# Two transformer blocks on one core: the same four attention beats in every stage, and the pool inputs of the second block projected first

## The chip, the cores and the metric

The program runs on one core of one Trainium2 chip. The core has TensorE (PE in the profile, with its weight loads as PEld), VectorE (DVE), ScalarE (ACT), GpSimd (POOL) and SyncE (SP, which here only issues transfers). Each engine works through its own list of instructions in order and waits on semaphores for the others. The metric is the device time of the whole program in microseconds.

## The reference

The input is one sequence of 512 tokens with 1024 features. A first block has three attention branches that are gated and merged, and an MLP; then a second block runs twice (two layers), each a SwiGLU, a mixer with three branches, and another SwiGLU. What the change touches are the attention stages and the projections beside them:

```
# first block
oa = diff_attention(...)      # p0 - lam * p1, 4 heads of two parts
ob = banded_attention(...)    # window of 128, with a sink
oc = nsa_attention(...)       # compressed + selected + windowed branch, gated
# second block, for each of two layers
ya = chunked_relpos_attention(qa, ka, va, ..., rel_bias)
yb = multiscale_pool(ub, w_pool, pool_scale)       # windows 2, 4, 8, 16
yc = forgetting_attention(qc, kc, vc, ..., f_lin + forget_bias)
branch = einsum('bsnw,nwd->bsnd', stack([ya, yb, yc]), w_branch)
merged = sum(sigmoid(g) * branch)
```

## The kernel before, in words

Everything stays in SBUF transposed (features on partitions, 512 tokens in a row); weights stream in from memory through eight buffers. Products are made in three passes of single rounded parts: GpSimd splits each weight piece into `w_hi` and `w_lo` (L1119, L1122), and TensorE runs three matmuls for each block of 128 rows (L1151 to L1153). A "group" is one 128-column output: 8 such blocks, 24 matmuls, put down in pieces of two blocks (6 matmuls), so that other work can stand between pieces.

One list, `ORDER`, is written by `plan()` before the program is built. Each engine's program walks this list and emits its own part of every step. So the list fixes the order on every engine.

Attention runs as a pipeline over "duos" (two heads, one block of 128 queries). Stages in order of time: `att_a` (98 to 239 us of the trace, 16 duos), `att_b` (239 to 349 us, 16 duos), `att_c` (349 to 592 us, 48 duos, since each of the 16 has three branches), and for each layer of the second block `att_a2` (first layer 1502 to 1690 us) and `att_c2` (first layer 1690 to 1852 us), 16 duos each. A duo n goes through these steps:

- score: PE makes the scores (L1224) into banks 0 and 1, once the row maxima of duo n-1 are taken; DVE adds the bias and takes maxima (L1597) and negates them (L1602); ACT exponentiates (L1379).
- prob: DVE inverts the row sums (L1608) and scales the rows (L1634).
- turn: PE transposes the probabilities (L1241) into banks 2 and 3.
- copy: ACT moves them to SBUF, `pt_sb` (L1394). There is one `pt_sb`, so this waits for the pv of duo n-1.
- pv: PE multiplies by the values (L1266, L1253, L1261) into bank 4.
- At the last duo of a pair, bank 4 is moved out: `bout` is an ACT copy of the high part (L1467) and a DVE subtraction for the low part (L1812); in `att_a` it is a square and copy on ACT (`new_root`, "differential"). The pv of the next pair waits for that.

`attend()` returns a list of beats, each with a weight, and `weave()` deals out pieces of projection groups between beats in proportion to the weight. A "normed" group (query or key projection) is followed by a chain: square on ACT (L1353), a sum over channels on PE (L1210, into bank 5), a square root on ACT (L1361), two half reciprocals on DVE (L1557) and the scaled result on DVE (L1572). Only this last step gives the group's own bank back. `late()` holds these steps and lets one go after each piece. A "plain" or "token" group is just copied out by ACT.

Groups and pool products take banks in turn from a small ring: `MIX_RINGS` gives (6, 7) for `att_a2`, `att_c`, `att_c2`, and (3, 6, 7) for `att_a`, `att_b`. A pool product (`pool_steps`, PE L1323) also takes a place in the ring.

In `layer()` the stage `att_a2` has 17 groups: f (8 columns, for the forget gate), four u groups (pool input), four q and four k (normed), four token groups of values. `forget` is a small chain ACT, DVE, ACT in which ACT stands still while DVE works (L1412 to L1418, L1744 to L1753). `pool_steps` gives shifts, a last step (DVE) and a product.

Of the kernel before, what the change touches and what calls it, by code (L numbers as in the profile page):

```python
# [73 lines left out]
def put(*step):  # L74
    ORDER.append(step)
# [412 lines left out]
def attend(kind, layer):  # L488
# [20 lines left out]
    def turns(j):  # L509
        if 0 <= j + 1 < n:  # L510
            u = duos[j + 1]
            u.t_before = [take(b) for b in (T_BANKS[:1] if kind in ("att_a", "att_b") else T_BANKS)]
            for b in T_BANKS[:len(u.t_before)]:
                HELD[b] = ("pt_copied", u.n)
            put("turn", u)

    def products(j):
        if 0 <= j:
            u = duos[j]
            if u.first:  # L520
                u.o_before = take(O_BANK)
            u.need_v = READY[V_AT[kind]]
            put("pv", u)
        if 0 <= j and duos[j].last:
            u = duos[j]
            if kind == "att_a":
# [9 lines left out]
                masks.remove(e)  # L536
                mask_bias(e[1])

    def copy(j):
        if 0 <= j + 1 < n:  # L540
            put("copy", duos[j + 1])

    def scale(j):
        if j + 2 < n:
            put("prob", duos[j + 2])
# [1 line left out]
    out = []  # L547
    for j in range(-2, n):
        w = 1 + max([d.blocks for d in duos[max(0, j):j + 3]])
        if kind in ("att_b", "att_c", "att_c2"):  # L550
            out += [(lambda j=j: (scores(j), products(j)), 2 * w), (lambda j=j: (turns(j), copy(j)), w),
                    (lambda j=j: scale(j), w)]
        else:
            out += [(lambda j=j: scores(j), w), (lambda j=j: turns(j), w), (lambda j=j: (products(j), copy(j)), w),
                    (lambda j=j: scale(j), w)]
    return out + [(lambda: [mask_bias(b) for _, b in masks], 0)]


# [239 lines left out]
def layer(l, m):  # L798
# [12 lines left out]
    f = plain((l, "f"), ("f",), ring, width=8)  # L811
    q = [normed((l, "qc", i), "query", (l, 2), ("r2", i), ring) for i in range(4)]
    k = [normed((l, "kc", i), "key", (l, 3), ("r2", 4 + i), ring) for i in range(4)]

    steps = [pool_steps(g, ring) for g in range(4)]
    groups = [q[0], u[0], k[0], u[1], q[1], u[2], k[1], u[3], q[2], k[2], *token_groups((l, "vc"), S, "v1", ring),
              q[3], k[3]]
    jobs, chain = [f], []
    for g in groups:
        jobs += [g] + chain[:2]  # L820
        chain = chain[2:]
        if g is u[0]:
            jobs.append(forget)
        if g in u:
            shifts, product = steps[u.index(g)]
            chain += shifts + [product]
    jobs += chain
    weave("att_a2", l, jobs)
    ring = MIX_RINGS["att_c2"]
    weave("att_c2", l, merge((l + 1, 1), "br_b", "set", ring) + merge((l + 1, 0), "br_a", "mid", ring))  # L830
# [1161 lines left out]
```

How the kernel before makes its waits and increments, by code:

```python
    def wait_ge(self, name, n):  # L928
        if n > self.seen.get(name, 0):
            self.e.wait_ge(self.sem[name], n)
            self.seen[name] = n
# [1 line left out]
    def wait_at(self, at):  # L933
        if at:
            self.wait_ge(*at)
# [1 line left out]
    def settle(self):  # L937
        self.n += 1
        self.e.wait_ge(self.sem[self.chain], self.n)
# [139 lines left out]
        @block.sync  # L1080
        def _(sp):
            E = Engine(sp, sem, "out_done")
            for c in range(0, KC, 2):
                sp.dma_start(x[:, c, :], x_in[:, c, :]).then_inc(sem[f"x_loaded{c}"], 16)
            for p, piece in enumerate(PIECES):
                if p >= NR:
                    E.wait_ge("w_used", p - NR + 1)
                src = weights[AT[p] - piece.cols * P:AT[p]].rearrange("(p n) -> p n", p=P)
                sp.dma_start(raw[:, p % NR, 0:piece.cols], src).then_inc(sem[f"loaded{p % NR}"], 16)
            for d in range(KC):
                E.wait_ge("x_added", TOTAL["x_added"] - KC + d + 1)
                sp.dma_start(out[:, d, :], x[:, d, :]).then_inc(sem["out_done"], 16)
            sp.wait_ge(sem["out_done"], 16 * KC)
# [17 lines left out]
            def split(h):  # L1111
                p = SPLITS[h]
                n = PIECES[p].cols
                piece, high = raw[:, p % NR, 0:n], w_hi[:, h % NH, 0:n]
                if h >= NH:
                    E.wait_ge("w_used", SPLITS[h - NH] + 1)
                E.wait_ge(f"loaded{p % NR}", 16 * (p // NR + 1))
                nc.gpsimd.tensor_tensor(high, piece, ones[:, 0:1].to_broadcast([P, n]), ALU.mult)\
```

## Time and profile before

| | us |
|---|---|
| median of 3 runs | 3600.44 (3597.36 to 3603.72) |
| the profiled execution, its own time | 3600.44 |
| its span, first to last instruction | 3598.6 |
| PE busy | 3435.6 (95%) |
| GpSimd busy | 2371.3 (66%) |
| DVE busy | 1427.4 (40%) |
| ACT busy | 772.4 (21%) |
| chain that ended last | PE 87%, DVE 8%, ACT 3%, issue 2% |

The chain that ended last is the path of instructions and waits that ends with the last instruction. A row of waits says which engine stood idle, before which line, and which line's end let it go. A timeline row gives start and length, then the engine, line and operation with output and inputs by name, and in brackets the idle time before it. The slices of the page show where PE is not full: the first six of forty slices (the first block's attention), and a short dip in each layer of the second block.

### The profile page before, as it was taken

The numbers are of one execution on the slowest core, as the hardware profiler recorded it, in microseconds if no ns is written. First come the engines' busy times: TensorE is split into PE (matmuls) and PEld (weight loads), VectorE is DVE, ScalarE is ACT, GpSimd is POOL, SyncE is SP. The second block draws the span as 40 slices with busy tenths as digits, with TensorE's granted clock in tenths as the row PEclk, the third lists the DMA queues.
The fourth block names the chain that finished last, engine by engine and source line by source line (L and its number), as shares of the span: only waits on it lengthen the run. The fifth ranks groups of instructions, "written<-read, shape, count | busy, mean of one in ns | idle before, by whom it ended". The sixth has DMA issues, their size and how long they took to land.

```text
span 3598.6 us, 42372 instructions
## 1 busy us (share of the span) xinstructions
PE 3435.6 (95%) x17034; PEld 2751.9 (76%) x17034; DVE 1427.4 (40%) x2757; ACT 772.4 (21%) x1568; POOL 2371.3 (66%) x1238
## 2 busy tenths in 40 slices
PE   7876999999999999989999999999999889999999
PEld 6554667888898888656779888888887567788887
DVE  5656564433453234565333111332345653332111
ACT  2544332211120002243212100210012432111000
POOL 6413445787768776644677877787775436688775
PEclk9988999999999999999999999999999999999999
DMA  3212122254525442211222322254432112232222
GB/s 138 66 59 71 59 65 80 96 210 164 187 104 223 171 164 100 77 59 59 94 94 94 106 97 96 88 205 168 165 129 71 65 50 89 79 106 94 99 94 76
DMA packets 104195, 388.08 MB, mean 108 GB/s; under 512 B 11824, under 2 KB 12080, under 8 KB 97856
## 3 DMA queue, kind: packets, MB, share of 16 engines
q1 hardware_dynamic: 87984, 292.76, 24.2%
q10 hardware_dynamic: 16016, 92.62, 6.7%
q8 instruction: 135, 2.21, 0.3%
q14 instruction: 60, 0.49, 0.0%
HBM read 383.20 MB, written 2.13 MB: 107 GB/s over the span
## 4 chain that ended last, share of the span: by engine, by line
PE 87%; DVE 8%; ACT 3%; issue 2%; DMA 0%; ACTq 0%; DVEq 0%
PE psum L1151 27%; PE psum L1152 26%; PE psum L1153 26%; PE psum L1224 2%; PE psum L1266 2%; PE psum L1241 2%; DVE rs_t L1557 2%; DVE s_sb L1597 1%; PE psum L1210 1%; ACT s_sb L1379 1%; DVE neg_max L1602 1%; DVE s_sb L1634 1%; ACT sq_t L1353 0%; DMA small<-first_small_dram 0%; ACT L1361 0%
## 5 line engine op out<-in xcount | busy, mean ns | idle before, releaser
L1119 POOL TENSOR_TENSOR w_hi<-raw,ones 128x1024 fp32r<-128x1024 f32 (+3 forms) x591 | 1043.0, 1765 | 1064.7 <-PE psum L1153 1055.5
L1122 POOL TENSOR_TENSOR w_lo<-raw,w_hi 128x1024 fp32r<-128x1024 f32 (+3 forms) x591 | 1314.5, 2224 | 46.5
L1151 PE MATMUL psum<-h_hi,w_hi 128*128 128x512 f32 (+2 forms) x2912 | 1143.5, 393 | 29.8 <-DVE r L1572 17.5
L1153 PE MATMUL psum<-h_hi,w_lo 128*128 128x512 f32 (+2 forms) x2912 | 1108.1, 381 | 0.0
L1152 PE MATMUL psum<-h_lo,w_hi 128*128 128x512 f32 (+2 forms) x2912 | 1107.9, 380 | 0.0
L1151 PEld LDWEIGHTS psum<-h_hi,w_hi 128*128 128x128 f32 (+1 forms) x2912 | 552.0, 190 | 167.2 <-issue 34.2
L1153 PEld LDWEIGHTS psum<-h_hi,w_lo 128*128 128x128 f32 (+1 forms) x2912 | 551.4, 189 | 106.6
L1152 PEld LDWEIGHTS psum<-h_lo,w_hi 128*128 128x128 f32 (+1 forms) x2912 | 552.7, 190 | 101.0 <-issue 6.3
L1151 PE MATMUL psum<-a_hi,w_hi 128*128 128x512 f32 (+1 forms) x1064 | 392.5, 369 | 0.0
L1152 PE MATMUL psum<-a_lo,w_hi 128*128 128x512 f32 (+1 forms) x1064 | 391.9, 368 | 0.0
L1153 PE MATMUL psum<-a_hi,w_lo 128*128 128x512 f32 (+1 forms) x1064 | 391.9, 368 | 0.0
L1824 DVE TENSOR_TENSOR psum<-g_sb,psum 128x512 f32<-128x512 f32 x120 | 83.5, 696 | 734.3 <-PE psum L1153 641.4
L1502 ACT ACTIVATE g_sb<-psum 128x512 f32<-128x512 f32 x120 | 71.7, 598 | 919.5 <-PE psum L1153 832.9
L1379 ACT ACTIVATE s_sb<-s_sb,neg_max 128x128 f32<-128x128 f32 (+6 forms) x272 | 140.7, 518 | 487.0 <-DVE neg_max L1602 486.9
L1833 DVE SCALAR_TENSOR_TENSOR x<-psum,res,x 128x512 f32<-128x512 f32 (+1 forms) x132 | 88.4, 669 | 357.6 <-PE psum L1153 357.6
L1557 DVE RECIPROCAL rs_t<-rs_t 128x256 f32<-128x256 f32 x110 | 187.2, 1730 | 101.5 <-ACT rs_t L1361 101.3
L1151 PEld LDWEIGHTS psum<-a_hi,w_hi 128*128 128x128 f32 x1064 | 200.6, 189 | 33.7
L1152 PEld LDWEIGHTS psum<-a_lo,w_hi 128*128 128x128 f32 x1064 | 200.6, 189 | 33.5
L1153 PEld LDWEIGHTS psum<-a_hi,w_lo 128*128 128x128 f32 x1064 | 200.6, 189 | 33.1
L1509 ACT ACTIVATE a_hi<-psum 128x512 fp32r<-128x512 f32 x120 | 71.8, 598 | 494.0 <-DVE psum L1824 494.0
L1597 DVE CUSTOM_DVE_ANT_0 s_sb<-psum,bias_t 128x128 f32<-128x128 f32 (+3 forms) x224 | 109.5, 489 | 169.5 <-PE psum L1224 119.6
L1695 DVE CUSTOM_DVE_ANT_0 ada_t<-ada_t,psum 128x1024 f32<-128x1024 f32 x144 | 167.7, 1215 | 0.0
(189 smaller groups left out, 3385.2 us busy)
## 6 DMA issues: line engine op xcount, KB each, us to landing
raw<-weights_dram SPq DMA_DIRECT2D x489, 512.0 KB, 3.4
ada_t<-ada_dram ACTq DMA_DIRECT2D x48, 1536.0 KB, 7.1
raw<-weights_dram SPq DMA_DIRECT2D x72, 256.0 KB, 2.6
raw<-weights_dram SPq DMA_DIRECT2D x32, 384.0 KB, 2.9
bias_t<-biases_dram ACTq DMA_DIRECT2D x36, 256.0 KB, 2.9
bias_t<-cum_dram ACTq DMA_DIRECT2D x16, 256.0 KB, 4.0
out_dram<-x SPq DMA_DIRECT2D x8, 256.0 KB, 2.0
raw<-weights_dram SPq DMA_DIRECT2D x4, 408.0 KB, 3.1
```

The lines of the kernel that those rows point to most:

```text
L1119: nc.gpsimd.tensor_tensor(high, piece, ones[:, 0:1].to_broadcast([P, n]), ALU.mult)\
L1122: nc.gpsimd.tensor_tensor(w_lo[:, p % NR, 0:n], piece, high.bitcast(F32), ALU.subtract)\
L1151: mm(dst, lh, rh, start=first, stop=False)
L1152: mm(dst, lh, rl, start=False, stop=False)
L1153: return mm(dst, ll, rh, start=False, stop=last)
L1224: ins = mm(bank(SCORE_BANKS[half], w), q, k, start=True, stop=u.kind != "att_c2")
L1379: ins = fn(to, s, ACT.Exp, bias=neg_max[:, r:r + 1], accum_out=row_sum[:, r:r + 1])
L1557: v.reciprocal(r, r).then_inc(sem["qk_inverse"], 1)
L1597: v.tensor_tensor_reduce(out=s[:, 0:w], in0=bank(SCORE_BANKS[half], w), in1=tile, scale=1.0, scalar=s[:, w:w + 1] if u.kind == "att_b" els ...
L1695: ins = v.tensor_tensor_reduce(out=part, in0=part, in1=c_bcast, scale=1.0, scalar=0.0, op0=ALU.mult, op1=ALU.add, accum_out=mod_raw[:, l, ...
L1824: v.tensor_tensor(bank(g.bank), g_sb[:, n % 2, :], bank(g.bank), ALU.mult)\
L1833: v.scalar_tensor_tensor(x[:, d, cs], bank(g.bank)[:, cs], res_of(which, d), x[:, d, cs], ALU.mult, ALU.add).then_inc(sem["x_added"], 1)
```

## The change

The first part is in `attend()`. Before, three kinds (`att_b`, `att_c`, `att_c2`) had three beats a duo: score of duo j+2 with pv of duo j, weight 2w; turn and copy of duo j+1, weight w; prob of duo j+2, weight w. The other two had four beats. Now all kinds have four: score, turn, pv, prob, each of weight w. And the copy of duo j+1 is put down inside `products`, right behind pv and ahead of what follows the last duo of a pair (`bout`, or the square and copy of `att_a`).

The second part is in `layer()`: the order of the 17 groups of `att_a2`. Before, u groups stood between q and k groups and the values ahead of q3 and k3. Now the order is f, u0, u1, u2, u3, q0, k0, q1, k1, q2, k2, q3, k3, and the four token groups, with the forget step behind u0 and the pool steps between groups from u1 on.

```
@@ attend
             put("pv", u)
+        if 0 <= j + 1 < n:
+            put("copy", duos[j + 1])
         if 0 <= j and duos[j].last:
...
-    def copy(j):
-        if 0 <= j + 1 < n:
-            put("copy", duos[j + 1])
...
         w = 1 + max([d.blocks for d in duos[max(0, j):j + 3]])
-        if kind in ("att_b", "att_c", "att_c2"):
-            out += [(lambda j=j: (scores(j), products(j)), 2 * w), (lambda j=j: (turns(j), copy(j)), w),
-                    (lambda j=j: scale(j), w)]
-        else:
-            out += [(lambda j=j: scores(j), w), (lambda j=j: turns(j), w), (lambda j=j: (products(j), copy(j)), w),
-                    (lambda j=j: scale(j), w)]
+        out += [(lambda j=j: scores(j), w), (lambda j=j: turns(j), w), (lambda j=j: products(j), w),
+                (lambda j=j: scale(j), w)]
@@ layer
-    groups = [q[0], u[0], k[0], u[1], q[1], u[2], k[1], u[3], q[2], k[2], *token_groups((l, "vc"), S, "v1", ring),
-              q[3], k[3]]
-    jobs, chain = [f], []
-    for g in groups:
-        jobs += [g] + chain[:2]
-        chain = chain[2:]
-        if g is u[0]:
-            jobs.append(forget)
-        if g in u:
-            shifts, product = steps[u.index(g)]
-            chain += shifts + [product]
-    jobs += chain
+    jobs = [f, u[0], forget, u[1], *steps[0][0], u[2], steps[0][1], *steps[1][0], u[3], steps[1][1]]
+    chain = [s for ss, prod in steps[2:] for s in ss + [prod]]
+    rest = [q[0], k[0], q[1], k[1], q[2], k[2], q[3], k[3]] + token_groups((l, "vc"), S, "v1", ring)
+    for i, g in enumerate(rest):
+        jobs.append(g)
+        jobs += chain[2 * i:2 * i + 2] if i < 11 else chain[2 * i:]
     weave("att_a2", l, jobs)
```

Lines of the changed kernel below its `layer()` stand 13 lower than before (L1210 is L1197, and so on).

**Place 1: `att_b`, end of its first pair, on PE.** L1224 is the score of duo 22, L1266 the pv of duo 20 (the last of its pair), L1210 the sum of a normed group, L1241 the turn of duo 21 (with the change L1211, L1253, L1197 and L1228). Before:

```order
L1224 MATMUL psum<-k_56,r_51 128x256 [waits row_max]
L1224 MATMUL psum<-k_56,r_51 128x256
L1266 MATMUL psum<-pt_sb,v_bc 64x128 [waits pt_copied]
L1266 MATMUL psum<-pt_sb,v_bc 64x128 x3
L1151 MATMUL psum<-h_hi,w_hi 128x512
L1152 MATMUL psum<-h_lo,w_hi 128x512
L1153 MATMUL psum<-h_hi,w_lo 128x512
L1151 MATMUL psum<-h_hi,w_hi 128x512
L1152 MATMUL psum<-h_lo,w_hi 128x512
L1153 MATMUL psum<-h_hi,w_lo 128x512
L1210 MATMUL psum<-sq_t,cst 128x512 [waits qk_rooted,qk_squared]
L1241 MATMUL psum<-cst,s_sb 128x128 [waits probs]
```

and with the change:

```order
L1211 MATMUL psum<-k_56,r_51 128x256 [waits row_max]
L1211 MATMUL psum<-k_56,r_51 128x256
L1228 MATMUL psum<-cst,s_sb 128x128 [waits pt_copied,probs]
L1228 MATMUL psum<-cst,s_sb 128x128 x3
L1138 MATMUL psum<-h_hi,w_hi 128x512
L1139 MATMUL psum<-h_lo,w_hi 128x512
L1140 MATMUL psum<-h_hi,w_lo 128x512
L1138 MATMUL psum<-h_hi,w_hi 128x512
L1139 MATMUL psum<-h_lo,w_hi 128x512
L1140 MATMUL psum<-h_hi,w_lo 128x512
L1197 MATMUL psum<-sq_t,cst 128x512 [waits qk_rooted,qk_squared]
L1253 MATMUL psum<-pt_sb,v_bc 64x128 x4
```

The pv of the pair's last duo stood right behind the score; now it stands behind the turn, a piece of the projection and the sum.

**Place 2: the same place on ACT.** L1467 (now L1454) is the first half of `bout`, L1394 (now L1381) the copy of duo 21, L1361 (now L1348) the square root of the normed group. Before:

```order
L1467 ACTIVATE br_b<-psum 128x512 [waits pv]
L1353 ACTIVATE sq_t<-psum 128x512 [waits w_used]
L1361 ACT_TABLE_LOAD
L1361 ACTIVATE rs_t<-psum,eps_t 128x512 [waits qk_summed]
L1394 ACTIVATE pt_sb<-psum 128x2x256 [waits transposed]
```

and with the change:

```order
L1340 ACTIVATE sq_t<-psum 128x512 [waits w_used]
L1348 ACT_TABLE_LOAD
L1348 ACTIVATE rs_t<-psum,eps_t 128x512 [waits qk_summed]
L1381 ACTIVATE pt_sb<-psum 128x2x256 [waits pv,transposed]
L1454 ACTIVATE br_b<-psum 128x512
```

The `bout` copy went from the front of this run to its end, behind the square, the table load, the root and the copy. Its DVE half (L1812) keeps its place in DVE's list, ahead of the scaling of duo 22.

**Place 3: `att_a2`, the third pool product (PE).** L1323 (now L1310) is the pool product, behind it the first matmuls of the next normed group, k2 before and k1 with the change. Before:

```order
L1210 MATMUL psum<-sq_t,cst 128x512 [waits qk_rooted,qk_squared]
L1241 MATMUL psum<-cst,s_sb 128x128 [waits pt_copied,probs]
L1241 MATMUL psum<-cst,s_sb 128x128 x7
L1323 MATMUL psum<-pool_d,lay 128x512 [waits plain_out,pool_in]
L1151 MATMUL psum<-h_hi,w_hi 128x512 [waits w_lo,qk_out]
L1152 MATMUL psum<-h_lo,w_hi 128x512
```

and with the change:

```order
L1197 MATMUL psum<-sq_t,cst 128x512 [waits qk_rooted,qk_squared]
L1253 MATMUL psum<-pt_sb,v_57 64x128 x8
L1310 MATMUL psum<-pool_d,lay 128x512 [waits qk_out,pool_in]
L1138 MATMUL psum<-h_hi,w_hi 128x512 [waits w_lo,qk_out]
L1139 MATMUL psum<-h_lo,w_hi 128x512
L1140 MATMUL psum<-h_hi,w_lo 128x512
```

In both, the group behind the product has the same bank (7) as the normed group ahead of it, since the product took bank 6 between them, and waits for `qk_out` (L1572) of that group. Before, the other three products stand behind a plain or token group. With the change the first two do, and the fourth stands behind k2, a normed group, with q3 behind it on k2's bank: the wait stands twice in each layer instead of once.

## Rows read from the trace of the kernel before

**Rows 1.** Busy time of each engine by stretch; PEclk is the granted clock

```profile
core 0: us, PE busy (x) PEld busy (x) DVE busy (x) ACT busy (x) POOL busy (x), PEclk, DMA share, GB/s
239.00:349.00 110.00, 76.67 (x422) 47.77 (x421) 69.59 (x181) 49.58 (x113) 33.20 (x28) 0.83 0.22 75
349.00:592.00 243.00, 228.28 (x1348) 161.35 (x1344) 145.50 (x466) 87.93 (x262) 107.85 (x72) 0.96 0.19 60
1502.00:1690.00 188.00, 161.99 (x785) 108.75 (x784) 112.48 (x210) 74.78 (x139) 86.11 (x47) 0.95 0.19 63
1690.00:1852.00 162.00, 160.81 (x866) 122.38 (x864) 60.80 (x141) 40.27 (x96) 101.90 (x65) 1.00 0.28 88
```

**Rows 2.** Waits of PE, 1502 to 1692 us: in total, times, longest

```profile
PE psum L1210 <- ACT sq_t L1353: 17.1, 8, 6.4
PE psum L1151 <- DVE r L1572: 6.5, 1, 6.5
PE psum L1224 <- DVE neg_max L1602: 1.6, 1, 1.6
PE psum L1241 <- DVE s_sb L1634: 0.8, 1, 0.8
```

**Rows 3.** Waits of PE, 239 to 349 us

```profile
PE psum L1241 <- DVE s_sb L1634: 6.9, 3, 3.2
PE psum L1266 <- ACT pt_sb L1394: 3.3, 5, 1.1
PE psum L1266 <- DVE br_b L1812: 2.4, 2, 1.6
```

**Rows 4.** Waits of PE, 349 to 592 us

```profile
PE psum L1241 <- DVE s_sb L1634: 7.0, 6, 2.3
PE psum L1266 <- ACT pt_sb L1394: 2.3, 3, 1.3
PE psum L1253 <- ACT pt_sb L1394: 1.2, 2, 0.7
PE psum L1266 <- DVE br_c L1812: 1.1, 2, 0.7
```

**Rows 5.** Timeline of ACT in that stretch: start, length, idle before it

```profile
1532.03 0.61 ACT L1412 ACTIVATE f_t<-f_t 8x512 f32<-8x512 f32 x1
1539.10 0.60 ACT L1394 ACTIVATE pt_sb<-psum 128x512 f32<-128x512 f32 x1 [3.79 <-DVE f_t L1753]
```

**Rows 6.** Timeline of ACT and DVE behind one query or key group

```profile
1584.22 0.60 ACT L1353 ACTIVATE sq_t<-psum 128x512 f32<-128x512 f32 x1 [1.29 <-PE psum L1153]
1584.83 1.28 ACT L1361 ACT_TABLE_LOAD   x1
1586.13 0.69 ACT L1361 ACTIVATE rs_t<-psum,eps_t 128x512 f32<-128x512 f32 x1
1586.92 1.75 DVE L1557 RECIPROCAL rs_t<-rs_t 128x256 f32<-128x256 f32 x1 [3.20 <-ACT rs_t L1361]
1591.01 0.75 DVE L1572 SCALAR_TENSOR_TENSOR r<-psum,lay,rs_t 128x512 f32<-128x512 f32 x1
```

**Rows 7.** DVE's L1602, 1502 to 1690 us: busy, mean ns; then shortest/median/longest

```profile
L1602 DVE TENSOR_SCALAR neg_max<-row_max 128x2 f32<-128x2 f32 x18 | 11.1, 614 | 0.6
L1602 DVE TENSOR_SCALAR neg_max<-row_max x18: 168/169/1848, 1503.6 to 1687.8; 128x2 f32<-128x2 f32 x18
```

**Rows 8.** Busy time by stretch, right behind three of PE's waits

```profile
1519.50:1524.00 4.50, 4.44 (x15) 3.14 (x16) 1.83 (x2) 1.98 (x3) 4.42 (x3) 0.62 0.01 5
1616.00:1619.00 3.00, 3.00 (x10) 1.91 (x10) 0.55 (x2) 0.00 (x0) 0.00 (x0) 0.53 0.00 0
1626.00:1629.00 3.00, 2.60 (x12) 1.82 (x12) 2.34 (x3) 2.32 (x3) 2.92 (x2) 1.00 0.70 251
```

**Rows 9.** Timeline of PE, one turn in that stretch

```profile
425.09 0.87 PE L1241 MATMUL psum<-cst,s_sb 128*128 128x128 f32 x6 [2.28 <-DVE s_sb L1634]
```

**Rows 10.** Timeline of DVE, the first subtraction of that stretch

```profile
279.24 0.69 DVE L1812 TENSOR_TENSOR br_b<-psum,br_b 128x512 fp32r<-128x512 f32 x1 [1.64 <-ACT br_b L1467]
```

## The prediction, made before the changed kernel ran

> **What bounds the kernel now.** I read the busy time by stretch first. TensorE is full nearly everywhere: in `att_c2` it works 160.8 of 162 us, so nothing about waits can be won or lost there [rows 1]. The change touches only the attention stages, and three kinds of them have room: `att_b` (76.7 of 110 us busy), `att_c` (228.3 of 243) and `att_a2` (162.0 of 188, once per layer) [rows 1]. Then I asked each of these for PE's waits. In `att_a2` they are 17.1 + 6.5 + 1.6 + 0.8 = 26.0 us a layer: eight waits of a group's channel sum for its square on ACT, the longest 6.4, and one of 6.5 for a bank that a normed group still holds [rows 2]. In `att_b` and `att_c` the turn waits for scaled probabilities (6.9 and 7.0) and the pv for its copy or for the output bank (3.3 + 2.4 and 2.3 + 1.2 + 1.1) [rows 3, 4]. Last comes what stands around these waits on ACT and DVE. Elsewhere the program is word for word the same.
>
> **Part 1, the order of groups in `att_a2`.** No instruction is added; 17 groups of 24 matmuls, 16 duos, 8 sums and 4 pool products stay. Only waits change.
>
> What goes. The 6.4 us wait is ACT standing in `forget`: it starts at 1532.03 and the copy behind it at 1539.10, 7.1 us, and the square of k0 is queued behind that and one duo's exponentials [rows 5]. With the change the group in that place is a plain one: no square, no sum. PE meets forget through the copy of duo 82 and the probabilities of duo 83, with a whole group (4 pieces of about 1.5), a pv and a score between, about 7.4 us. DVE's scaling of duo 83 stands behind forget's scan and takes 0.8; I leave 1.2 us (bounds 0 and 6.4). The 1.6 us at the stage's end goes, since the last normed group is four token groups earlier.
>
> What comes. First the waits at the start: 0.8 as before, 1.2 for forget, and 0.5 each where u3 and q0 take the bank of the plain group ahead, 3.0 together. Each of eight normed groups costs at least 0.7, the square of 0.60 and the hand-over [rows 6]: 5.5. Now eight of them stand in a row, so I set the chain against PE's slot. From a group's end: square 0.60, table load 1.28, root 0.69, half reciprocal 1.75, one duo's scaling 0.8, the other half 1.75, result 0.75 [rows 6], then a duo's maxima (0.8 to 1.7) and exponentials (0.9 to 1.5), and only then the next square: 9.3 to 10.8 us. PE's slot (wait, sum, four pieces, one score, turn and pv) is 9.1 to 10.5. In four slots chain and slot meet within 0.3; in three, where a score has no turn behind it or a subtraction stands between, walking through the list gives 2.2, 1.2 and 1.2. With 0.3 for the others that is 4.9.
>
> Then the bank. A wait on a normed group's bank now comes twice. From the group's end the result is out after about 7.5 us (the same chain without maxima and exponentials), and PE has 3.7 us of sum, pv or turn, and pool product in front: 3.8 each, 7.6 (bounds 2 and 6.5, the latter the wait of before [rows 2], which had a late square ahead of it).
>
> GpSimd splits weights all the time, and the little negation of two columns takes 169 ns or up to 1848, 614 in the mean [rows 7]. It is on the chain in each slot: 8 x (0.614 - 0.169) = 3.6.
>
> Sum of waits: 3.0 + 5.5 + 4.9 + 7.6 + 3.6 = 24.6 against 26.0. The clock comes on top. Behind the long waits PE's granted clock is between its two levels (1.2 and 2.4 GHz): 0.62 over 4.5 us, 0.53 over 3 us, after waits of 2.4 and 6.5; after one of 1.8 it is 1.00 [rows 8]. That is 1.7 and 1.4 us lost. Before there are four such waits, 6.2 us; after I count three (two banks and the 2.2 with its 0.7), 4.7. So 29.3 against 32.2: 2.9 less in a layer, 5.8 less in both. Bounds: without lateness and contention 16.1 + 3.1, 13 less in a layer; with bank waits of 6.5 and twice the contention 6 more.
>
> **Part 2, the beats in `att_b`, `att_c`, `att_c2`.** Two things follow. The turn of duo j+1 comes earlier after its probabilities: pv of duo j, and in many duos a piece of the projection, no longer stand between. Against that the pv comes later after its copy, and those waits go.
>
> `att_c`: I took each of the 48 turns, the time between its probabilities and its start, and the work that is moved behind it (0.4 to 2.4 us). In twelve of them the work is more than that time; the extra waits add up to 8.4. The largest is 2.2, the turn at 425.09, which waits 2.28 already [rows 9]; the others are 0.2 to 1.1. The pv waits of 2.3 + 1.2 + 1.1 = 4.6 go [rows 4]: 3.8 more.
>
> The output subtraction. It stands in DVE's list ahead of a duo's scaling, and waits for ACT's `bout` copy, that waits for the pair's last pv. Before, that pv is right behind the score, and the subtraction starts at 279.24 after 1.64 us of waiting [rows 10]. Now turn, projection piece and at the first pair of `att_b` also a channel sum stand ahead on PE, and square, load, root and copy on ACT. Walking on, the pv ends near 281.1, copy and `bout` near 282.4, the subtraction near 283.1: 3.2 us later than 279.93, where its end was. DVE's list slips with it. At other pairs it is 0.5 to 1.2 in `att_b`, where the exponentials hold ACT anyway, and up to 3 in `att_c`, where most disappears in slack. For `att_b`, where PE waits on DVE, I take 2.0 + 0.5 + 1.2 = 3.7 and nothing for its turns (they fall into other waits on DVE) nor for pv waits. For `att_c` I take 2.5 besides the 3.8: 6.3. Bounds: -3 to +8 and -3 to +14.
>
> `att_c2`: the turns have 3.8 us or more and lose at most 3.8; nothing. `att_a`: the copy, 0.60 [rows 5], now stands ahead of the square at a pair's end; four times, mostly beside a projection piece: 1.0 (0 to 2.4). GpSimd's and SP's lists don't change but for the places of masks, that nobody waits for; the order in which weights come follows the groups, at the same bytes.
>
> **Sum.** -5.8 + 3.7 + 6.3 + 1.0 = +5.2. The profiled execution took 3600.4 us, 1.8 more than its span, and is the median itself. So 3605.6; I say 3605.
>
> **A rule weighed.** In [rows 6] the load ends at 1586.11 and the root begins at 1586.13. The Trainium skill, "ScalarE: Activation LUTs", section "What ACT_TABLE_LOAD costs", states 1.28 us and a drain of 1.38 on top for each switch. By that page's figures, an estimate, each chain of the eight in a row would be 1.4 longer, about 20 us over two layers. The load agrees with the trace, the drain doesn't show in it, and this gets no chance.
>
> **The rivals.**
> A, faster: the projections win. Chains stay inside PE's slots, as four of eight group ends in `att_a2` now cost only 0.7, and contention misses them: -13 a layer. For it speaks that slots and chain are equal within a microsecond; against it that [rows 7] has a mean three times the shortest. With half of part 2 (5): 3600.4 - 26 + 5 = 3579.
> B, slower: the subtraction decides. If each of the eight pair ends in `att_b` and `att_c` costs the 3.2 of the first, it is 26 instead of 6.2: 3605 + 20 = 3625. It decides from the point where the next scaling has less than 3.2 us before its turn; in [rows 9] it has none. Against it: DVE is busy only 60% of these stretches.
> C, slower: GpSimd on DVE's chain in `att_a2`. At the longest row, 1.68 more each of eight times, it is 13.4 instead of 3.6, 20 us over both layers: 3625; with half of the slots 3615. The Trainium skill, "SBUF — State Buffer", section "SBUF: two separate sides", has the port pair as an exclusive lock held for a whole instruction, by which such a hit lasts to the end of GpSimd's; the longest row fits.
> D: the waits in part 2 only change places, and it nets to nothing: 3600.4 - 5.8 + 1 = 3596.
>
> **How the numbers follow.** A measurement here can tell 0.2%, 7.2 us, from nothing: 3593 to 3608. My forecast and D lie in it, together 0.40. A has 0.22, B 0.24, C 0.14. So faster 0.22, same 0.40, slower 0.38. The range takes in most of A's way down and B and C: 3586 to 3625; the forecast's own is 3596 to 3613.
>
> **What would show it.** In `att_a2`: no 6.4 us wait behind forget, two waits on `r` (L1559 of the changed kernel) near 3.8, eight waits for squares, three of them above 1.5, a stage of about 185 us. In `att_b`: the first subtraction (L1799) near 282.4 instead of 279.2. In `att_c`: pv waits gone, turn waits near 13. I am wrong if the bank waits are gone or above 6, if `att_c` gets shorter, or if `att_c2` moves at all.

## The result, and the profile after

The changed kernel takes 3640.2 us (median of 4, 3638.3 to 3644.3) against 3601.6 (3597.4 to 3603.7) for the kernel before in the same session: ratio 1.011, 95% interval 1.0093 to 1.0128. It is slower, and outside the range I gave (3586 to 3625). The profiled execution took 3637.6 us, with a span of 3635.8.

Busy time by stretch in the changed kernel, in order of time: `att_a`, `att_b`, `att_c`, and the first layer's `att_a2` and `att_c2`, cut where each one's first score starts:

```profile
core 0: us, PE busy (x) PEld busy (x) DVE busy (x) ACT busy (x) POOL busy (x), PEclk, DMA share, GB/s
98.70:236.30 137.60, 112.95 (x521) 82.03 (x520) 92.19 (x178) 71.28 (x137) 52.91 (x35) 0.96 0.20 63
236.30:353.30 117.00, 75.13 (x423) 46.19 (x422) 72.75 (x180) 49.03 (x111) 33.19 (x28) 0.85 0.20 69
353.30:608.00 254.70, 234.83 (x1346) 158.69 (x1344) 156.62 (x466) 88.36 (x263) 107.89 (x72) 0.97 0.18 58
1519.50:1705.50 186.00, 154.25 (x739) 102.93 (x738) 103.07 (x196) 74.93 (x135) 77.34 (x41) 0.93 0.17 58
1705.50:1878.60 173.10, 171.89 (x914) 127.98 (x912) 70.73 (x155) 42.37 (x102) 111.64 (x71) 1.00 0.28 88
```

Set against the kernel before, in us. Each stage begins at its first score and lasts to that of the next; `att_c` and `att_c2`, behind which other work follows, end with their last pv (so `att_c2` is 1.6 shorter here than its window above):

| stage | before | after | change |
|---|---|---|---|
| `att_a` | 141.2 | 137.6 | -3.6 |
| `att_b` | 109.3 | 117.0 | +7.7 |
| `att_c` | 242.9 | 254.7 | +11.8 |
| `att_a2`, two layers | 176.2, 174.7 | 186.0, 185.9 | +9.8, +11.2 |
| `att_c2`, two layers | 170.6, 170.6 | 171.5, 171.5 | +0.9, +0.9 |

They add up to 38.7; the spans differ by 37.2, and what lies between the stages is 1.5 shorter. All but `att_a` came out positive.

How far can a single stage length be trusted? `att_b` and `att_c` have the same program in the changed kernel and in three runs that come below, `e1`, `e7` and `r9`. There `att_b` takes 119.7, 119.8 and 119.8 instead of 117.0, and `att_c` 254.6, 259.4 and 254.8 instead of 254.7. The waits are the same (41.9 to 42.1 us in `att_b` in all four); what differs is PE's busy time in `att_b` (75.1 against 77.7) with the granted clock of the stretch (0.85 against 0.83). So a stage length can be off by 3 us or more for the clock alone, while the sums of waits nearly repeat (with the old program of `att_b` 33.3 before, 33.4 in `e3` and 32.6 in `o1`), and the loss of `att_b` is nearer 10 than 7.7.

PE's waits in `att_a2` of the changed kernel (total, times, longest), the counterpart of [rows 2]:

```profile
PE psum L1138 <- DVE r L1559: 12.8, 2, 7.1
PE psum L1197 <- ACT sq_t L1340: 11.1, 8, 3.7
PE psum L1228 <- DVE s_sb L1621: 7.5, 3, 6.1
```

31.4 us, against 24.4 in the same cut before (the 26.0 of [rows 2] has a wait of 1.6 behind it, which belongs to `att_c2`). The waits for squares fell from 17.1 to 11.1, as meant. But the bank waits are 7.1 and 5.6 where I had 3.8 each, and the turn behind forget waits 6.1 (I had 1.2). PE's busy time rose too, from 151.8 to 154.3 with the same 739 matmuls: behind the waits of 6.1 and 7.1 the 512-column matmuls take 0.63 us instead of 0.39. In `att_b` and `att_c` (two queries, against [rows 3, 4]):

```profile
PE psum L1228 <- DVE s_sb L1621: 16.4, 8, 6.1
PE psum L1211 <- DVE neg_max L1589: 9.0, 4, 6.2
PE psum L1197 <- ACT sq_t L1340: 8.7, 4, 6.1
PE psum L1297 <- ACT cmp_g L1460: 7.8, 1, 7.8
```

```profile
PE psum L1228 <- DVE s_sb L1621: 13.9, 10, 4.7
PE psum L1211 <- DVE neg_max L1589: 3.1, 1, 3.1
PE psum L1226 <- DVE s_sb L1621: 2.8, 2, 1.8
```

Before, `att_b` also had these beside those of [rows 3], and `att_c` the same wait of 3.1 for its first row maxima:

```profile
PE psum L1224 <- DVE neg_max L1602: 11.3, 5, 6.2
PE psum L1310 <- ACT cmp_g L1473: 5.3, 1, 5.3
PE psum L1210 <- ACT sq_t L1353: 4.1, 4, 1.6
```

The waits of pv are gone in both. In `att_b` all waits together rose from 33.3 to 41.9: turns 9.5 more, squares 4.6 more, the last row (the gate of the next stage) 2.5 more, scores 2.3 less and pv 5.7 less. In `att_c` the turns wait 16.7 instead of 7.0, and all waits together rose from 14.7 to 19.8 us. This rise of 5.1 is less than half of the stage's 11.8. The rest is busy time: the PE column of its window is 234.8 instead of 228.2, with the same 1346 matmuls and a granted clock that is no lower (0.97 against 0.96). A view of waits alone doesn't show that.

### The profile page after: what moved, and what is told of

The parts are those of the page before. It is cut to its first block, busy times and chain, and to the rows that moved or that the text cites. A ratio compares the mean times of both kernels' runs of the same rounds, so it can differ in the third digit from the quotient of the medians.

```text
span 3635.8 us, 42471 instructions
## 1 busy us (share of the span) xinstructions
PE 3447.4 (95%) x17034; PEld 2746.0 (76%) x17034; DVE 1442.9 (40%) x2757; ACT 777.5 (21%) x1572; POOL 2373.3 (65%) x1238
## 3 DMA queue, kind: packets, MB, share of 16 engines
q1 hardware_dynamic: 87984, 292.76, 23.6%
## 4 chain that ended last, share of the span: by engine, by line
PE 86%; DVE 8%; ACT 3%; issue 2%; DMA 0%; ACTq 0%; DVEq 0%
PE psum L1138 27%; PE psum L1139 26%; PE psum L1140 26%; PE psum L1211 2%; PE psum L1253 2%; PE psum L1228 2%; DVE rs_t L1544 2%; DVE s_sb L1584 1%; PE psum L1197 1%; ACT s_sb L1366 1%; DVE neg_max L1589 1%; DVE s_sb L1621 1%; ACT sq_t L1340 0%; DMA small<-first_small_dram 0%; ACT L1348 0%
## 5 line engine op out<-in xcount | busy, mean ns | idle before, releaser
L1138 PEld LDWEIGHTS psum<-h_hi,w_hi 128*128 128x128 f32 (+1 forms) x2912 | 552.5, 190 | 191.0 <-issue 41.9
L1139 PEld LDWEIGHTS psum<-a_lo,w_hi 128*128 128x128 f32 x1064 | 200.6, 188 | 33.3
L1140 PEld LDWEIGHTS psum<-a_hi,w_lo 128*128 128x128 f32 x1064 | 200.5, 188 | 33.3
L1584 DVE CUSTOM_DVE_ANT_0 s_sb<-psum,bias_t 128x128 f32<-128x128 f32 (+3 forms) x224 | 109.4, 488 | 173.3 <-PE psum L1211 126.0
```

What stands on the lines that cost most here:

```text
L1138: mm(dst, lh, rh, start=first, stop=False)
L1139: mm(dst, lh, rl, start=False, stop=False)
L1140: return mm(dst, ll, rh, start=False, stop=last)
L1584: v.tensor_tensor_reduce(out=s[:, 0:w], in0=bank(SCORE_BANKS[half], w), in1=tile, scale=1.0, scalar=s[:, w:w + 1] if u.kind == "att_b" els ...
```

## The experiments

All stage lengths below are cut as in the table above, and each is from one execution. Each ratio is against the kernel before in the same session (its medians were 3598.9 to 3600.5). Everything not named is as in the kernel that a run starts from.

### Which part, which stage

`e1_beats_alone` has the new beats and the old groups, `e2_groups_alone` the new groups and the old beats. `e3_copy_in_a` moves only the copy in `att_a` and `att_a2`:

```
             put("pv", u)
+        if kind in ("att_a", "att_a2") and 0 <= j + 1 < n:
+            put("copy", duos[j + 1])
```

`e4_beats_old_copy` has the four beats with the copy where it was, `e5_pv_first_even` four even beats with pv ahead of the turn (the lines are shortened):

```
-            out += [(lambda j=j: (scores(j), products(j)), 2 * w), (lambda j=j: (turns(j), copy(j)), w), ...
+ e4         out += [(scores, w), (turns, w), (products and copy, w), (scale, w)]
+ e5         out += [(scores, w), (products, w), (turns and copy, w), (scale, w)]
```

> Part 2 and the early copy alone: four beats of equal weight in all five kinds, the copy right behind pv; groups of att_a2 in their old order. Theory (the parts add up): att_a 137.6 us, att_b 117.0, att_c 254.7, att_c2 173.1 as in the changed kernel, att_a2 near 176; sum 3600 - 3.6 + 7.7 + 11.7 - 1.0 = 3615, ratio 1.004. Rival (the two parts only hurt together, since the place of groups and beats against each other decides): under 3605, with att_c below 248.

> The new order of groups in att_a2 alone, beats as before. Theory (the parts add up): att_a2 near 186 us in both layers, its forget wait near 6 and its two bank waits near 7 and 5.6 stay; 3600 + 21 = 3621, ratio 1.006. Rival (the early copy makes the forget wait, as the copy of duo 83 then stands in front): forget wait under 3, att_a2 near 180, 3608.

> Only the copy's place in the two four-beat kinds att_a and att_a2: right behind pv, ahead of the square of a pair's end. Theory: att_a 137.6 us instead of 141.2, att_a2 within 1 of 176.2; 3597, ratio 0.999. Rival (the gain in att_a came from something else, such as the phase of GpSimd's splits): att_a within 1 of 141.2, 3600.

> Four beats in att_b, att_c, att_c2, but the copy behind the output copy as before, in all kinds; old order of groups. Theory (the turn moved ahead of the piece and of pv decides, not the copy): att_b near 117, att_c near 254, att_a 141.2; 3619, ratio 1.005. Rival (the place of the copy ahead of the output copy delays the subtraction and makes the loss): att_b near 110, att_c near 244, 3601.

> The kernel before with four equal beats in att_b, att_c and att_c2, but pv still ahead of the turn (score, pv, turn and copy, prob, one weight each). It tells the order from the spread of the pieces. Theory (what costs is that a turn stands ahead of pv, so that it comes sooner after its probabilities): att_b 109 to 111, att_c 242 to 245, att_c2 170.6; 3600 to 3604. Rival (the equal spread of the projection's pieces costs, whichever of the two comes first): att_b near 114, att_c near 254, 3613.

| run | us; ratio, 95% interval | `att_a` | `att_b` | `att_c` | `att_a2` | `att_c2` |
|---|---|---|---|---|---|---|
| before | 3600.0 | 141.2 | 109.3 | 242.9 | 176.2, 174.7 | 170.6 |
| e1 | 3623.2; 1.0063 (1.0048 to 1.0078) | 138.7 | 119.7 | 254.6 | 176.2, 176.8 | 173.1 |
| e2 | 3614.9; 1.0040 (1.0025 to 1.0055) | 137.9 | 109.4 | 242.3 | 185.1, 186.3 | 169.0 |
| e3 | 3602.4; 1.0004 (0.9994 to 1.0014) | 143.5 | 109.8 | 243.0 | 177.6, 174.7 | 170.6 |
| e4 | 3613.1; 1.0041 (1.0028 to 1.0054) | 137.9 | 113.6 | 253.9 | 174.8, 174.8 | 173.1 |
| e5 | 3607.5; 1.0016 (1.0006 to 1.0025) | 137.9 | 115.9 | 243.2 | 176.5, 174.9 | 173.2 |

The parts add: 0.63% and 0.40% make 1.03% of the 1.1%. The rival of e1 fell, though e1 came out 8 us above the 3615 that I had added up from single stage lengths, and e2 6 us below its 3621. The rival of e2 fell too: without the early copy, forget's wait is still 6.1 and the bank waits 7.1 and 5.6.

The 3.6 of `att_a` is no effect of the change that these runs could show. The stage has the same program before and in e2, e4 and e5, and takes 141.2 us in the first and 137.9 in the other three; e3 with the copy moved takes 143.5. My expectation for e3 missed. With its program unchanged the length ranges from 137.2 to 144.7 over the runs here, and the granted clock from 98.5 to 236 us is 0.96 in the shortest (o2), 0.93 before, and 0.89 in the longest (o1).

In `att_c` the order decides. The copy's place is worth 0.7 (e4, 253.9), within the scatter, the even spread 0.3 (e5); the turn ahead of pv is worth 10.7. In `att_b` it is the other way round, and there I go by the waits, since they repeat: 33.3 before, 38.8 in e5, 38.9 in e4 and 42.1 in e1. So the even spread makes 5.5, the turn ahead of pv nothing, and the early copy 3. Here the rival of e5 was right, and the theory of e4 (near 117) missed. `att_c2` takes 2.5 from the beats and gives 1.6 back with the groups, as the wait at its start goes.

### The wait behind forget

`e7_forget_in_four` starts from the changed kernel:

```
-    jobs = [f, u[0], forget, u[1], *steps[0][0], u[2], steps[0][1], *steps[1][0], u[3], steps[1][1]]
+    jobs = [f, u[0], lambda: forget(0), u[1], *steps[0][0], lambda: forget(1), u[2], steps[0][1], *steps[1][0],
+            lambda: forget(2), u[3], steps[1][1], lambda: forget(3)]
```

> The changed kernel with forget cut into four steps at four places (sum and ACT's three functions behind u0; DVE's three small operations ahead of u2; the scan ahead of u3; ACT's store behind u3). Theory (the 6.1 us wait is DVE's scan in front of a scaling, and ACT's wait for it inside forget in front of a copy): the wait goes to under 2, att_a2 185.9 to about 179 in each layer with the clock behind it; 3640 - 13 = 3627. Rival (the wait is GpSimd on DVE's port, which meets whatever operation stands there): at least 4 of the 6.1 stay, in the scaling or the scan; 3636.

Measured: 3627.5 us, 1.0071 (1.0056 to 1.0086), `att_a2` 179.1 and 178.8: 6.9 and 7.1 less than in the changed kernel. The turn behind forget doesn't wait any more, two later ones wait 0.3 and 0.4, and a bank waits 1.9 for ACT. The time is the theory's. But that the wait goes when the operations stand apart doesn't say why they took so long together, and there the rival had a part. DVE's timeline of the changed kernel shows it (start, length, operation), with two rows of GpSimd behind it:

```profile
1540.02 2.40 DVE L1734 TENSOR_SCALAR f_t<-f_t 8x512 f32<-8x512 f32 x1 [4.44 <-ACT f_t L1403]
1542.45 0.68 DVE L1736 TENSOR_TENSOR f_t<-f_t 8x512 f32<-8x512 f32 x1
...
1543.88 2.08 DVE L1740 TENSOR_TENSOR_SCAN f_t<-f_t 8x512 f32<-8x512 f32 x1
...
1546.05 2.46 DVE L1621 TENSOR_SCALAR s_sb<-s_sb,row_inv 128x256 f32<-128x256 f32 x2
1542.52 2.37 POOL L1106 TENSOR_TENSOR w_hi<-raw,ones 128x1024 fp32r<-128x1024 f32 x1 [0.38 <-PE psum L1140]
1544.96 3.13 POOL L1109 TENSOR_TENSOR w_lo<-raw,w_hi 128x1024 fp32r<-128x1024 f32 x1
```

The first took 0.41 before, the scan 1.21, and the scaling is 0.62 where nothing stands against it. The three are 4.7 longer, and my 1.2 plus 4.7 is 5.9 of the 6.1 measured. But for 0.4 us ahead of 1542.52, GpSimd splits weights in all this time. With the splits made short (e8, next) the same turn waits 0.8, for ACT, though forget stands whole. So the 6.1 needs both: three operations in a row, and GpSimd beside them.

### GpSimd against DVE

`e8_after_short_splits` and `e9_before_short_splits` make the two split operations short, in the changed kernel and in the one before. They leave out the low part of the weights: TensorE reads the high part in its place, with as many matmuls, waits and transfers:

```
-                n = PIECES[p].cols
+                n = PIECES[p].cols if h < 24 else 32
-                nc.gpsimd.tensor_tensor(w_lo[:, p % NR, 0:n], piece, high.bitcast(F32), ALU.subtract)\
+                nc.gpsimd.tensor_tensor(rest[:], piece[:, 0:32], high[:, 0:32].bitcast(F32), ALU.subtract)\
-                        wh, wl = w_hi[:, h % NH, w], w_lo[:, p % NR, w]
+                        wh, wl = w_hi[:, h % NH, w], w_hi[:, h % NH, w]
```

> The changed kernel with GpSimd's two split operations cut to 32 columns (the high part is kept from the first pieces, the low part is left out and the high one read in its place): GpSimd is all but idle, every wait and every transfer stays. With the next kernel it tells how much of the change's loss is GpSimd on DVE. Theory G (GpSimd's hits make a third or more of it): changed less before comes to under 26 us instead of 38; att_c differs by under 7 instead of 11.8, att_a2 by under 7 instead of 10 to 11, and forget's wait is near 2. Theory O (the order of PE alone): the differences stay as they are within 2 us.

> The kernel before with the same short splits (the same part left out). Both theories: DVE's operations of 0.2 us are never 1 us or longer, and the kernel is faster than 3600 by what GpSimd costs it: by the DVE waits of PE in the attention stages 20 to 60 us. Theory G: it gains less from this than the changed kernel does, 12 us or more less; theory O: both gain the same.

| | `att_b` | `att_c` | `att_a2` | `att_c2` | all |
|---|---|---|---|---|---|
| e9, before, short | 102.4 | 230.2 | 165.6, 165.1 | 169.9 | 3570.7 |
| e8, after, short | 104.5 | 239.4 | 174.6, 173.2 | 170.7 | 3597.4 |
| difference | 2.1 | 9.2 | 9.0, 8.1 | 0.8 | 26.7 |
| with full splits | 7.7 | 11.8 | 9.8, 11.2 | 0.9 | 38.6 |

Against its own session the kernel before is 30 us faster with short splits, the changed one 43. That is a net number: in the profiled executions the seven attention stages together are 48 us shorter in e9 and 58 in e8, but the rest of the program is 19 and 17 us longer, though PE is full and hardly waits there. Why is open, so the two runs are not a clean removal of GpSimd. Of the change's loss the splits make 12 us: 5.6 of 7.7 in `att_b`, 2.6 in `att_c`, and 0.8 and 3.1 in `att_a2`. Theory G just missed its own signs (26.7 where it wanted under 26, 31% where it wanted a third), and missed by stage, where I had expected under 7 in `att_c` and `att_a2`; theory O, that nothing changes by more than 2, missed by far more (the changed kernel gains 13 us more than the other, G's 12 or more). The bank waits are the same to 0.1 with short splits, so they come from the order of the lists:

```profile
PE psum L1139 <- DVE r L1560: 12.7, 2, 7.1
PE psum L1198 <- ACT sq_t L1341: 10.0, 8, 2.6
```

Which of DVE's operations are hit? Two lines of equal size in the kernel before, all 144 duos (duration min/median/max in ns):

```profile
L1602 DVE TENSOR_SCALAR neg_max<-row_max x144: 168/170/2222, 99.9 to 3099.5; 128x2 f32<-128x2 f32 x144
L1608 DVE RECIPROCAL row_inv<-row_sum x144: 99/165/167, 101.8 to 3103.7; 128x2 f32<-128x2 f32 x144
```

The reciprocal is never longer than 167 ns; the negation goes up to 2222. Counted in the trace, the negation started inside a running split 60 times and was lengthened by over 0.4 us in 42 of them. The length says more: all 53 that started with over 0.17 us of the split to go ended 22 to 30 ns behind the split's end, and the 84 that started outside of a split took 172 ns at most. So the operation waits for the end of GpSimd's. Of the scalings by `row_inv` (L1634), those of 128 and 256 columns were lengthened 28 times in 28, those of 384 and 512 in 14 of 20. The reciprocals (L1608, L1557) were never lengthened in 106 such starts, nor was `scalar_tensor_tensor` with an input in PSUM (L1543) in 89. The Trainium skill, "SBUF — State Buffer", section "SBUF: two separate sides", names the operations that take part in the lock on the port pair that the two engines share: a DVE operation in a 2-port mode or with two inputs in SBUF. The trace agrees as far as these kinds go.

In `att_b` two hits in a row show how it comes about. DVE and GpSimd in the changed kernel, from 331 us:

```profile
331.77 2.32 DVE L1621 TENSOR_SCALAR s_sb<-s_sb,row_inv 128x256 f32<-128x256 f32 x2
...
335.26 1.13 DVE L1589 TENSOR_SCALAR neg_max<-row_max 128x2 f32<-128x2 f32 x1
332.05 1.89 POOL L1106 TENSOR_TENSOR w_hi<-raw,ones 128x1024 fp32r<-128x1024 f32 x1 [15.09 <-PE psum L1140]
334.02 2.35 POOL L1109 TENSOR_TENSOR w_lo<-raw,w_hi 128x1024 fp32r<-128x1024 f32 x1
```

The piece of the projection ends at 331.97, which frees GpSimd's slot; its split starts at 332.05, inside a scaling that takes 2.32 instead of 0.62, and the next catches the negation (1.13 for 0.17). ACT's exponentials and the square behind them slip, and the channel sum waits 6.1 us. In e8 the same wait is 3.5, shorter by the 2.6 that the two hits add.

### The negation on ACT

`r12_before_negation_on_act`:

```
-                v.tensor_scalar(neg_max[:, r:r + 2], row_max[:, r:r + 2], -1.0, None, ALU.mult)
+                fn(neg_max[:, u.at:u.at + 2], row_max[:, u.at:u.at + 2], ACT.Copy, scale=-1.0)   # in exps()
```

> The kernel before with the negation of the maxima (two columns, 0.17 us or up to 1.8 on DVE) moved to ACT, in all 144 duos. Theory (this little operation waits for the end of a GpSimd split in 42 of 144 cases, 47 us in all, and a part of it is on PE's path): DVE's excess falls by over 40 us, PE's waits in att_b, att_c and att_a2 by 8 to 15; 3588. Rival (what DVE is spared there, its next scaling or ACT's extra operation, 0.2 us each, pays): 3598 to 3606.

Measured: 3602.1 us, 1.0004 (0.9996 to 1.0013). The rival was right. DVE's excess, each operation's time above the median of its line and shape, fell from 143 to 106 us: the negations' 47 went, and the scalings behind them were hit harder (58 to 64). But PE gained nothing by it in sum. `att_c` is 4.1 shorter, `att_a2` 1.1 and 2.2 longer, and there the added operation stands on ACT, for whose squares PE waits. What part of the rest each of the two pays was not told apart.

### The banks behind a product

DVE in the changed kernel behind the longest bank wait, and ACT's operation ahead of it:

```profile
1602.25 0.69 ACT L1518 ACTIVATE br_b<-psum,lay 128x512 fp32r<-128x512 f32 x1 [0.60 <-PE psum L1310]
1602.97 0.75 DVE L1835 SCALAR_TENSOR_TENSOR br_b<-psum,lay,br_b 128x512 fp32r<-128x512 f32 x1 [5.41 <-ACT br_b L1518]
1603.64 0.14 DVE L1707 COPY pool_s<-r 128x1 f32<-128x1 f32 x1
1603.82 0.69 DVE L1709 TENSOR_TENSOR pool_s<-r 128x511 f32<-128x511 f32 x1
1604.54 1.75 DVE L1544 RECIPROCAL rs_t<-rs_t 128x256 f32<-128x256 f32 x1
...
1606.75 1.75 DVE L1544 RECIPROCAL rs_t<-rs_t 128x256 f32<-128x256 f32 x1
1608.54 0.75 DVE L1559 SCALAR_TENSOR_TENSOR r<-psum,lay,rs_t 128x512 f32<-128x512 f32 x1
```

The root of the group whose bank PE waits for was done at 1600.95. DVE took it up at 1604.54: its list has the product's output (L1835) and a pool shift ahead of the reciprocals, and L1835 waits for PE's product and ACT. That is 3.6 us on top of the chain I had walked, and with my 3.8 it makes 7.4 for the 7.1 measured.

`r9_products_late`, from the changed kernel:

```
-    chain = [s for ss, prod in steps[2:] for s in ss + [prod]]
+    chain = steps[2][0] + steps[3][0]
...
-        jobs += chain[2 * i:2 * i + 2] if i < 11 else chain[2 * i:]
+        jobs += chain[2 * i:2 * i + 2]
+        if i in (8, 10):
+            jobs.append(steps[2 + (i == 10)][1])
```

`r10_before_forget_in_four` splits forget in the kernel before. `r11_groups_repaired` takes the old beats, the new groups, r9's products and e7's forget.

> The changed kernel with pool products 2 and 3 moved from the run of normed groups to the token groups; their shifts stay where they are. Theory (a product takes one of the two banks, so that the next normed group has to take that of the group just ended, and DVE's list has the product's output, which waits for PE and ACT, ahead of that group's reciprocals): both bank waits, 7.1 and 5.6, go, and with them the low clock behind them; att_a2 185.9 to 170 to 173 in each layer, 3640 - 28 = 3612. Rival (the chain of square, root, reciprocals is as long as PE's slot, so the time comes back as later squares): waits for squares rise by 5 or more, att_a2 179 to 183, 3630.

> The kernel before with forget in four steps (behind u0, k0, u1 and q1). Theory (the 6.4 us wait is ACT held in forget by its wait for DVE's scan): it goes to under 1.5, att_a2 176.2 to 168 to 171 with the clock behind it; 3600 - 12 = 3588, ratio 0.997. Rival (DVE, lengthened by GpSimd, then delays the scaling instead): att_a2 above 173, 3596.

> The beats of before, the new order of groups, with products 2 and 3 late and forget in four steps: both causes of att_a2's loss taken away. Theory: att_a2 186 - 6.9 - 14 = 165 in each layer against 176.2 and 174.7 of before; 3600 - 20 = 3580, ratio 0.9945. Rival (eight normed groups in a row are dear in themselves): att_a2 172 or more, 3595.

| run | us | ratio, 95% interval | `att_a2` |
|---|---|---|---|
| r9 | 3614.9 | 1.0041 (1.0028 to 1.0054) | 172.1, 172.0 |
| r10 | 3593.1 | 0.9979 (0.9970 to 0.9988) | 172.7, 171.3 |
| r11 | 3572.6 | 0.9928 (0.9915 to 0.9940) | 162.5, 162.6 |

r9's theory holds: 13.9 us a layer, and the squares rose by 0.8, not 5. It takes away two things at once, the product's turn on the bank ring and its output in DVE's list, and no run parts them; the 3.6 above is the share that the timeline gives to the list. r10 gave less than expected: the wait of 6.4 is 1.8, but a bank waits 1.8 and a turn 1.1 behind it. r11 beats both kernels. PE's waits in its `att_a2`:

```profile
PE psum L1210 <- ACT sq_t L1353: 11.9, 8, 3.7
PE psum L1151 <- ACT r L1370: 1.9, 1, 1.9
PE psum L1241 <- DVE s_sb L1637: 1.5, 3, 0.8
```

Against r10, which has the old order of groups and forget in four too, r11's `att_a2` is 10.2 and 8.7 shorter. So the order of groups is good; it was the two steps inside it that cost.

### PE's own time

Three rows of `att_c`, first e5 (pv first), then e4 (turn first), then e8 (turn first, short splits); the fourth is e9, the kernel before with short splits:

```profile
352.40:595.60 243.20, 229.80 (x1346) 158.72 (x1344) 152.50 (x466) 87.47 (x262) 107.90 (x72) 0.97 0.20 60
350.00:603.90 253.90, 234.69 (x1346) 158.61 (x1344) 157.65 (x466) 88.42 (x262) 107.96 (x72) 0.98 0.19 58
336.70:576.10 239.40, 231.62 (x1346) 156.96 (x1344) 111.49 (x466) 89.09 (x262) 18.30 (x69) 0.99 0.20 61
336.30:566.50 230.20, 224.10 (x1346) 159.04 (x1344) 111.18 (x466) 88.97 (x262) 18.17 (x68) 0.99 0.21 64
```

The same 1346 matmuls keep PE busy 4.9 longer if turns stand first, and 7.5 longer in e8 than in e9, where its waits differ by 2.0 (7.7 and 5.7 summed). I cut the trace of `att_c` into runs of matmuls of one kind, from a run's first start to the next run's first start, idle time off: before, the 48 turns take 18.5, after 23.6; the pieces 150.5 and 152.4 (in 83 and 90 runs); scores and pvs together 59.3 and 58.9. Before, 46 of 48 turns had a piece behind them, after 24, and 24 a pv. Turns of equal size show the same: a turn of two matmuls takes 0.14 us between two pieces (e5 and e4), 0.19 to 0.20 with a score or pv ahead and a piece behind, 0.32 with a piece ahead and a pv behind, and 0.39 with a score ahead and a pv behind.

`att_c2` has hardly a wait, so it was the place to tell apart the number of visits and what follows what:

```
+        if kind == "att_c2":
+ o1         out += [(lambda j=j: (scores(j), turns(j), products(j), copy(j), scale(j)), 4 * w)]
+ o2         out += [(lambda j=j: (scores(j), products(j), turns(j), copy(j), scale(j)), 4 * w)]
```

> The kernel before, in att_c2 alone one beat of weight four: score, turn, pv in a row, then all of the duo's pieces. Theory V (PE pays 0.09 us for each separate visit, as 28 more of them made 2.5): one visit a duo instead of two, att_c2 168 us instead of 170.6 in each layer. Theory N (it pays by which follows which; a turn in front of pv is dearer than one in front of a piece by about 0.12): 171 to 175.

> The same with score, pv, turn in a row. Theory V: 168 us, as with the turn first. Theory N: 170 to 171, 1 us or more less than with the turn first.

```profile
1678.40:1849.00 170.60, 167.85 (x903) 127.62 (x901) 69.30 (x157) 42.81 (x102) 101.48 (x66) 1.00 0.26 82
1688.80:1861.90 173.10, 170.37 (x909) 127.05 (x907) 71.07 (x157) 43.22 (x102) 102.91 (x66) 1.00 0.27 82
1683.40:1852.40 169.00, 167.11 (x903) 127.54 (x901) 73.49 (x157) 41.43 (x102) 101.93 (x66) 1.00 0.27 83
1674.90:1843.10 168.20, 166.32 (x903) 127.61 (x901) 74.93 (x157) 41.38 (x102) 101.67 (x66) 1.00 0.27 83
```

In this order: before (33 runs of pieces in the stage), e4 (47), o1 (17, turn first) and o2 (17, pv first). PE is busy 167.9, 170.4, 167.1, 166.3. But the matmul counts say that e4's stage isn't the same work: 909 against 903 in the others, one piece of six matmuls more before the last pv, and at 0.23 us each (the distance of two in the timeline) that is 1.4 of the 2.5. That piece is then missing behind the stage. From the first score of `att_c2` to that of the next `att_a2` the kernel before takes 1094.9 us, e4 1094.6 and the changed kernel 1094.4; from the second `att_c2` to the end it is 650.6, 651.6 and 650.0. So 14 more visits cost 1.1 in the stage (by the landmarks nothing in the first layer, 1.0 in the second), and 16 fewer in the same order (o2) give 1.5: 0.1 us each or a little less, and the change as a whole loses nothing there. The order counts as well: 15 turns in front of a pv cost 0.8 (o1 against o2). Each theory had half. o2 is 3591.4 us, 0.9980 (0.9970 to 0.9990), o1 0.9993 (0.9983 to 1.0003). In `att_c`, where the counts are equal, the order costs more, 4.9 for 24 turns; why four times as much per turn stays open. The profile models the ends of matmuls, and some of it may be short waits that hide under them.

`o3_repaired_and_negation` is r11 with r12's negation in `att_c` alone.

> The repaired kernel (beats of before, new groups, products late, forget in four steps) with the negation of the maxima on ACT in att_c alone. Theory (it took 4.1 us from att_c in the kernel before): 3568, att_c 238.7. Rival (another phase of GpSimd's splits against DVE gives it back): 3573.

Measured: 3570.8 us, 0.9919 (0.9905 to 0.9932). `att_c` is 240.8, not 238.7: 1.7 less than in r11, and by the total it can't be told from r11 (nor can its theory, 3568, be told from its rival, 3573).

## Why the prediction was wrong

The sum was +5.2 and is +38.6. Step by step:

- **`att_a2`, -2.9 a layer; measured +9.8 and +11.2.** (Of the 2.9, 1.6 was the last wait of [rows 2], which went and is counted in `att_c2` here.) The squares were a little better than forecast: 14.0 forecast with contention, 11.1 measured, three of eight above 1.5. The step that failed is "3.8 each" for the bank waits (12.8 instead of 7.6). I had walked the normed group's chain and not DVE's list, in which the product's output stands ahead of it and waits for two other engines. The second failed step is the 1.2 for forget: its cover is right with short splits (the turn waits 0.8 for its copy there in e8, and DVE's three operations take 0.41, 1.21 and 0.62), but three operations in a row were hit. Third, the clock: I had it give 1.5 back, and PE's busy time rose by 2.5, since the long waits were four (6.1, 7.1, 3.7 and 5.6) where I had counted three shorter ones. I had said that I am wrong if the bank waits are above 6, and one is.
- **Contention.** Rival C had GpSimd on the negations of eight chains. DVE's excess in `att_a2` fell instead, from 22 to 14 us. Three of the hits went to forget and the scaling behind it, where each counted.
- **`att_b`, +3.7; measured +7.7.** The mechanism is there. The first subtraction starts 42.6 us behind the stage's start instead of 39.5: 3.1 later, where I had worked out 3.2:

```profile
278.89 0.69 DVE L1799 TENSOR_TENSOR br_b<-psum,br_b 128x512 fp32r<-128x512 f32 x1 [4.62 <-ACT br_b L1454]
```

  With short splits the loss is 2.1, and in the full kernels the two hits at 331.77 and 335.26 make 2.6 of it. The term that was too small is the waits: 3.7 forecast, 8.6 measured, the turns behind DVE's list above all.
- **`att_c`, +6.3; measured +11.8.** The size of the waits was right: 5.1 more, the pv waits gone, turn waits 16.7 against my 13. The step that failed is that the sum had no term for PE's own time, which rose by 6.6. I had taken matmuls as costing the same in any order.
- **`att_c2`, 0; measured +0.9 a layer.** By my own rule, wrong if it moves at all, I was wrong there. But the stage's length is no loss: it has one piece more inside, and to the next landmark the changed kernel is 0.5 and 0.6 shorter. More visits cost up to 1.1, and the wait of 1.6 at its start went.
- **`att_a`, +1.0.** It can't be seen under a scatter of 137 to 145.
- **Rival B** (subtraction, 3.2 at each pair) did not decide: in `att_c` e4 and e1 are equal within 0.7, though one has the copy ahead of `bout` and the other behind it. That its total and C's, 3625, came nearest to 3640 says nothing for either. Rivals A and D were on the wrong side.

The chances gave 0.38 to slower, but the range ended at 3625: B and C each carried one mechanism, and what came was several at once: banks 5 and forget 5 more than forecast in each layer, with the low clock behind them, GpSimd's hits 8 in `att_b` and `att_c`, and PE's own time 6.6 in `att_c`.

## What to carry to other kernels

When a step is moved in a list, walk the list of each engine that serves the chain, not the chain alone: what stands ahead of it there may wait for a third engine. Look at busy time beside waits: in a row of small matmuls the order itself costs, and no wait shows it. DVE's operations meet GpSimd's by phase, so every move of work deals these hits anew; put work that can be hit three times in a row (as forget) into separate steps. And before a stage's length is taken for a loss, count its matmuls, compare its waits, and look at a landmark behind it.

## What the runs showed of the hardware

- GpSimd's splits lengthen DVE's `tensor_scalar`, `tensor_tensor` and copies between SBUF tensors (0.17 up to 2.2 us for a negation of two columns, to within 30 ns of the split's end), and never its reciprocals or its `scalar_tensor_tensor` with an input in PSUM: 0 of 195 counted. The attention stages of the kernel before are 48 us shorter with short splits, the whole program 30.
- A separate visit of PE to the projection costs about 0.1 us, with the same matmuls. A turn of two matmuls takes 0.14 us between pieces of the projection and 0.39 between a score and a pv.
- The same program's first attention stage took 137.2 to 144.7 us in single executions of different kernels, with a granted clock of 0.96 down to 0.89 in its stretch. A gain of 3.6 there can't be told from nothing.
